# Weight sums made a group ahead, and low parts of streamed weight chunks made by an accumulating load onto the negated high part

## What is computed

```python
x = layer_norm(ALPHA * x + 0.5 * swiglu(x, ffn1_w_up, ffn1_w_down), ln1_g, ln1_b)
h, new_buf, S_new = mixer(x, pos, conv_buf, S0, w_in, conv_w, w_conv_br, w_ret_br, w_out)
x = layer_norm(ALPHA * x + h, ln2_g, ln2_b)
x = layer_norm(ALPHA * x + 0.5 * swiglu(x, ffn2_w_up, ffn2_w_down), ln3_g, ln3_b)

def swiglu(x, w_up, w_down):
    a, b = jnp.split(x @ w_up, 2, axis=-1)
    return (jax.nn.silu(a) * b) @ w_down
```

## Time and profile before

| what | us |
|---|---|
| median of 3 runs | 1880.46 |
| lowest and highest | 1879.18, 1884.25 |
| the profiled execution | 1879.75 |
| its span, first to last instruction | 1877.9 |
| PE busy (share of the span) | 1786.2 (95%) |
| DVE busy | 1445.9 (77%) |
| ACT busy | 674.4 (36%) |
| POOL busy | 641.2 (34%) |

### The profile page before, as it was taken

One profiled execution on the slowest core, in us unless ns is written; L12 is line 12 of the kernel. 1 busy time (PEld: TensorE's weight loads), 2 busy tenths in 40 slices (PEclk: granted clock), 3 DMA queues, 4 the chain that ended last, 5 costly groups with the idle time before them and its releaser, 6 DMA issues. The chain is left out here.

```text
span 1877.9 us, 27089 instructions
## 1 busy us (share of the span) xinstructions
PE 1786.2 (95%) x10680; PEld 1654.4 (88%) x10680; DVE 1445.9 (77%) x1860; ACT 674.4 (36%) x1160; POOL 641.2 (34%) x427
## 2 busy tenths in 40 slices
PE   9979797989999999999999999999999989898898
PEld 9959696979999999999998989888889878788797
DVE  7978787778988777787266777787868878787976
ACT  5415151424344454444105050505224424232333
POOL 3433334353242222222242323131442444343531
PEclk9989998999999999999999999999999999999999
DMA  8746473753454343433674949495951747464633
GB/s 305 224 135 205 143 222 115 224 168 101 180 157 135 99 138 102 146 105 99 236 254 150 336 150 348 154 329 221 362 178 57 224 148 222 138 218 140 190 111 101
DMA packets 99038, 341.34 MB, mean 182 GB/s; under 512 B 9953, under 2 KB 10337, under 8 KB 98401
## 3 DMA queue, kind: packets, MB, share of 16 engines
q1 hardware_dynamic: 51552, 185.36, 28.9%
q0 software_dynamic: 22192, 81.27, 15.7%
q10 hardware_dynamic: 25168, 72.99, 10.7%
HBM read 298.35 MB, written 75.83 MB: 199 GB/s over the span
## 5 line engine op out<-in xcount | busy, mean ns | idle before, releaser
L852 POOL TENSOR_TENSOR wl<-raw,wh 128x1024 fp32r<-128x1024 f32 x124 | 327.4, 2644 | 146.3 <-DMA wh<-in_weights 48.8
L983 PE MATMUL ps<-th,wql 128*128 128x320 f32 x1136 | 351.3, 309 | 1.9 <-ACT pu L1705 1.9
L983 PE MATMUL ps<-th,wqh 128*128 128x320 f32 x1136 | 350.7, 309 | 0.0
L983 PE MATMUL ps<-tl,wqh 128*128 128x320 f32 x1136 | 350.0, 308 | 0.0
L878 POOL TENSOR_TENSOR quad_s<-qraw 128x512 f32<-128x512 f32 x71 | 98.0, 1380 | 605.8 <-DVE wql L2187 386.8
L983 PE MATMUL ps<-xh,wql 128*128 128x320 f32 x852 | 263.4, 309 | 0.8 <-DVE ct L2187 0.5
L983 PE MATMUL ps<-xl,wqh 128*128 128x320 f32 x852 | 262.7, 308 | 0.0
L983 PE MATMUL ps<-xh,wqh 128*128 128x320 f32 x852 | 262.6, 308 | 0.0
L1705 ACT ACTIVATE pu<-ps 128x320 f32<-128x320 f32 x213 | 93.0, 437 | 441.5 <-PE ps L983 441.5
L2187 DVE TENSOR_TENSOR wql<-qraw,wqh 128x512 fp32r<-128x512 f32 x213 | 249.8, 1173 | 0.4
L2187 DVE TENSOR_TENSOR wql<-quad_s,wqh 128x512 fp32r<-128x512 f32 (+1 forms) x213 | 199.0, 934 | 47.0 <-ACT wqh L1705 46.3
(11 more groups left out here) (294 smaller groups left out, 3816.2 us busy)
## 6 DMA issues: line engine op xcount, KB each, us to landing
qraw<-in_quads SPq DMA_DIRECT2D x142, 512.0 KB, 3.7
raw<-in_weights SPq DMA_DIRECT2D x92, 512.0 KB, 5.1
wh<-in_weights POOLq DMA_DIRECT2D x84, 512.0 KB, 5.8
raw<-sums_scratch SPq DMA_DIRECT2D x32, 512.0 KB, 3.7
wh<-sums_scratch POOLq DMA_DIRECT2D x32, 512.0 KB, 5.7
state<-in_state_ret ACTq DMA_DIRECT2D x32, 512.0 KB, 7.7
out_ret_sample<-state ACTq DMA_DIRECT2D x32, 512.0 KB, 5.1
sums_scratch<-in_sum_add POOLq DMA_DIRECT2D x8, 1024.0 KB, 10.0
```

The costliest lines, as they stand in the source:

```text
L852: pool.tensor_tensor(w_lo(r), w_raw(r), w_hi(r).bitcast(f32), ALU.subtract).then_inc(chunk_split, 1)
L983: ins = nc.tensor.matmul(out, lhs, rhs, start=start, stop=stop, skip_group_check=adds)
```

## The change

**Low parts.** For the chunks that are not in BY_ACT, SP no longer loads raw. POOL waits for the high part, writes its negative into wl (line 851 of the new kernel), waits for that instruction, and issues a DMA that loads the plain numbers with an add onto what stands in wl (line 854), so that wl becomes raw - wh. Each slot has a semaphore low_loaded, for which PE waits instead of chunk_split. The nine BY_ACT chunks keep the load by SP and the subtraction.

**Sums.** The adds for a group are issued one group earlier: those of the first group before the loop, those of group n+1 inside group n. ACT's base_copy moves with them: it now stands behind the last quad of a group, for the group two later, and once behind the first quad of all. The last of the three adds now stands among the down products, between the loads of A22's high part and the low part of S3. The calls of high, low and sums in the loop stand in another order.

**SP.** Its queue now holds the quads' loads almost alone; it waits no more for chunk slots or for the sums, except for the BY_ACT chunks.

```diff
@@ -686,8 +688,9 @@
                 for _ in range(n):
                     c = ck.at
                     r = slot_of(c)
-                    slot_free(sync, c)
-                    sync.dma_start(w_raw(r), chunk_source(sync, c)).then_inc(raw_loaded[r], 16)
+                    if c in BY_ACT:
+                        slot_free(sync, c)
+                        sync.dma_start(w_raw(r), a["weights"][PLAIN[c]]).then_inc(raw_loaded[r], 16)
                     ck.add()
 
             def load_quad(stage):
...
@@ -724,13 +727,9 @@
                     load(FIRST_UNITS)
                 load(2)
                 for g in SPLIT_GROUPS:
-                    load(1)
-                    load_quad(2 * k)
-                    load_quad(2 * k)
-                    load(1)
-                    load_quad(2 * k)
-                    load(2)
-                    load_quad(2 * k)
+                    for _ in range(4):
+                        load(1)
+                        load_quad(2 * k)
                     load(3)
                 load(2)
                 load_quad(2 * k)
...
@@ -844,16 +842,23 @@
                 c = ck.at
                 high(c + 1)
                 r = slot_of(c)
-                pool.wait_ge(raw_loaded[r], 16 * loads_of_slot(c))
                 if c in BY_ACT:
+                    pool.wait_ge(raw_loaded[r], 16 * loads_of_slot(c))
                     pool.wait_ge(hi_made, BY_ACT.index(c) + 1)
+                    pool.tensor_tensor(w_lo(r), w_raw(r), w_hi(r).bitcast(f32), ALU.subtract).then_inc(chunk_split, 1)
                 else:
                     pool.wait_ge(hi_loaded[r], 16 * high_loads_of_slot(c))
-                pool.tensor_tensor(w_lo(r), w_raw(r), w_hi(r).bitcast(f32), ALU.subtract).then_inc(chunk_split, 1)
+                    pool.tensor_scalar(w_lo(r), w_hi(r).bitcast(f32), -1.0, None, ALU.mult).then_inc(high_negated, 1)
+                    nk.add()
+                    pool.wait_ge(high_negated, nk())
+                    pool.dma_start(w_lo(r), chunk_source(pool, c), accum_op=ALU.add,
+                                   max_dma_last_dim=4 * D).then_inc(low_loaded[r], 16)
                 ck.add()
 
             def add_first(at):
 
+                if at == SPLITS:
+                    return
                 pool.wait_ge(base_copied, 16 * (at + 1))
                 pool.dma_start(a["sums"][at, 0:2].rearrange("m p d -> (m p) d"),
                                a["sum_add"][at].rearrange("m p d -> (m p) d"), accum_op=ALU.add,
...
@@ -907,24 +914,28 @@
                 high(ck(2))
                 low()
                 low()
+                if k == 0:
+                    add_first(0)
                 sums(2 * k)
+                if k == 0:
+                    add_next(0, 1)
+                    add_next(0, 2)
                 for g in SPLIT_GROUPS:
-                    at = split_after(k, g)
-                    high(ck(1))
+                    following = split_after(k, g) + 1
+                    high(ck(3))
                     sums(2 * k)
-                    add_first(at)
                     low()
                     sums(2 * k)
-                    add_next(at, 1)
+                    add_first(following)
+                    low()
                     high(ck(2))
                     sums(2 * k)
-                    add_next(at, 2)
-                    high(ck(3))
                     low()
+                    add_next(following, 1)
                     sums(2 * k)
                     low()
-                    low()
                     high(ck(2))
+                    add_next(following, 2)
                     low()
                     high(ck(2))
                     low()
...
@@ -1001,10 +1012,12 @@
                 return b
 
             def chunk():
-                s = slot_of(ck.at)
+                c, s = ck.at, slot_of(ck.at)
                 ck.add()
-                if ck() > FIRST_HI:
-                    pe.wait_ge(chunk_split, ck(-FIRST_HI))
+                if c in BY_ACT:
+                    pe.wait_ge(chunk_split, BY_ACT.index(c) + 1)
+                elif c >= FIRST_HI:
+                    pe.wait_ge(low_loaded[s], 16 * high_loads_of_slot(c))
                 return s
 
             def idle_products(n, b):
...
@@ -1874,8 +1887,10 @@
                 for g in range(1, len(GROUPS)):
                     for q in range(4):
                         quad(QUAD_START[2 * k] + 4 * (g - 1) + q)
-                        if q == 2 and g in SPLIT_GROUPS and split_after(k, g) < 2 * len(SPLIT_GROUPS) - 1:
-                            base_copy(split_after(k, g) + 1)
+                        if q == 0 and (k, g) == (0, 1):
+                            base_copy(1)
+                        if q == 3 and g in SPLIT_GROUPS and split_after(k, g) + 2 < SPLITS:
+                            base_copy(split_after(k, g) + 2)
                     if (k, g) == (1, 1):
                         act.dma_start(a["y_prompt"][0:ADDED * 128, :], a["ln3_b"].to_broadcast([ADDED * 128, D])
                                       ).then_inc(y_biased, 16)
```

More of the change, by code:

```diff
@@ L39 @@
 SUMS_KEPT = ("S1", "S3", "S2", "S4")
+SPLITS = 2 * len(SPLIT_GROUPS)
 SPLIT_BANKS = 8
@@ L138, in loads_of_slot @@
 def loads_of_slot(c):
-    return sum(SLOTS[e] == SLOTS[c] for e in range(FIRST_HI, c + 1))
+    return sum(SLOTS[e] == SLOTS[c] and e in BY_ACT for e in range(FIRST_HI, c + 1))
 def high_loads_of_slot(c):
@@ L544, in build_layer @@
         hi_loaded = [sem(f"hi_loaded{i}") for i in range(NSPL + 2)]
-        chunk_split = sem("chunk_split")
+        chunk_split, high_negated = sem("chunk_split"), sem("high_negated")
+        low_loaded = [sem(f"low_loaded{i}") for i in range(NSPL + 2)]
         first_loaded = [sem(f"first_loaded{n}") for n in range(len(FIRST_LOADS))]
@@ L763, in projections @@
                 fourth = SECOND + FIRST_UNITS - 1
-                sync.wait_ge(raw_loaded[slot_of(fourth)], 16 * loads_of_slot(fourth))
                 sync.wait_ge(hi_loaded[slot_of(fourth)], 16 * high_loads_of_slot(fourth))
@@ L830, in _ @@
         def _(pool):
-            ck, hk, qk = Count(FIRST_HI), Count(FIRST_HI), Count()
+            ck, hk, qk, nk = Count(FIRST_HI), Count(FIRST_HI), Count(), Count()
             def high(n):
@@ L1941, in _ @@
                 quad_hi_part(PROJ, what)
-            act.wait_ge(chunk_split, FFN_CHUNKS - FIRST_HI)
+            act.wait_ge(low_loaded[slot_of(SECOND - 1)], 16 * high_loads_of_slot(SECOND - 1))
             ln_load(1)
```

## The result

| | before | after |
|---|---|---|
| median of 4 runs, us | 1880.35 | 1932.86 |
| lowest and highest | 1879.18, 1884.25 | 1927.85, 1937.46 |
| profiled span | 1877.9 | 1926.1 |
| mean granted clock | 0.979 | 0.966 |

The ratio is 1.0276, with a 95% interval of 1.0254 to 1.0299: 52.5 us slower, where 6.5 us faster was forecast, and outside the range.

A forecast was written before the change was run, and what follows sets the result against it. PE, busy 1786.2 of 1877.9 us, was taken to bound the kernel, its idle time mostly waits for DVE's z and ct. -23 - 3 + 17.5 + 2 = -6.5 us gave 1873.2, median 1874; range 1845 to 1902.

The forecast's parts named there:

- The stop ahead of S1: PE's wait for ct before the down products' S1 goes in seven groups, 3.3 us each: 23 us gained.
- The negation: POOL's negation of a high part takes 1.3 us, bounds 1.3 to 2.6, as it reads half a subtraction's numbers.
- GpSimd's issues: By the skill's rule, the 121 loads moved to POOL cost perhaps 0.3 us more each where DVE is busy.
- The accumulating load: The low part's adding load lands in 5.5 to 6 us where DMA queues are quiet; bounds 3.7 and 14.0.
- Down products: From S1 to S4's end in eight split groups: S3 starts 6 us earlier, mostly lost again behind the base copy; -3 us.
- supply keeps up: Rival: the accumulating load lands in 5.6 us even beside the base copy, S4 starts at 22 us; about 1830, chance 0.12.
- Starts: Low parts without slack come late: opening +2.5 us, projections +5 and +1, second feed-forward stage +3.5, last chunk and conv +1.5.
- First group: POOL waits in line for the base copy and two adds before the third quad's sums, delaying DVE and PE: +4 us.
- Heads: Low parts in the heads have 5 us to spare: 0 us, with a bound of 5 us a head.
- Clock: One or two of the new stops bring PE's clock down behind them: +2 us.
- Late low parts: Rival: accumulating loads take 11 to 14 us as a rule, delaying heads, conv units and starts; about 1915, chance 0.18.
- the signs listed for "wrong": Negation above 2.4 us, middle landing below 4.5 or above 9, wl waits in heads, DVE over 10 us for POOL's sum.

The follow-up runs named there:

- no_negation: The changed kernel without the negation and its wait, for all but the first eight chunks and the extra slots (wrong numbers): 1927.7 us, ratio to before 1.0261.
- plain_load: The changed kernel with the low part's second load made plain, without the addition (wrong numbers), negation kept: 1876.4 us, ratio to before 0.9984.
- down_by_subtraction: The changed kernel with S3, A22 and S4 of the eight split groups (24 chunks) again loaded raw by SP and subtracted: 1891.9 us, ratio to before 1.0046.
- copy_next: The changed kernel with ACT's base copy moved behind the first quad of the next group: 1936.4 us, ratio to before 1.0295.
- starts_by_subtraction: The changed kernel with the chunks at the four starts again loaded raw by SP and subtracted: 1909.9 us, ratio to before 1.0155.
- heads_by_subtraction: The changed kernel with chunks from the fifth of the projections to the output projection's end loaded raw and subtracted (47 change): 1917.5 us, ratio to before 1.0209.
- lows_alone: The changed kernel with the sums' adds and base copies in the places and order of before, only low parts new: 1952.5 us, ratio to before 1.0366.

## Why the prediction was wrong, point by point

*The stop ahead of S1: right.* PE's wait for ct fell from 26.9 to 1.2 us, 3 to 4.4 us a group; 23 were forecast.

*The negation: mis-sized.* 3.0 us, outside my bounds of 1.3 to 2.6. The step that failed is the one by which half the reads mean half the time. The Trainium skill (GPSIMD Engine Reference, section 3.1) led the same way, to 0.9 to 1.5 us; the trace doesn't agree. It mattered little: no_negation won 5 us. My guess that GpSimd's issues would cost 0.3 us more a load came out in size (0.92 us against plain_load's 0.58), but it goes with the addition, not with where the load is issued.

*The accumulating load: right alone, wrong in company.* 5.4 us at best and 7.1 in the middle; 5.5 to 6 were forecast for quiet queues. What it adds to the DMA engines' work is 1.25 us, where the text had 1.4.

*Down products: this is where it failed.* -3 forecast; measured 282.1 - 248.6 = +33.5, of which down_by_subtraction gives back 38.0. Two steps failed. The first is S3's high part landing at about 5 us: it landed at 9.3, and still at 8.0 in the last group, with neither copy nor add behind it. The rest of the way to the issue was sized rightly in sum (3.2 us, 2.9 forecast), the long negation included. So even the two groups without a base copy behind them start on S3 at 19.7 and 16.9 us, not 14, and lose 3.7 us together where the text had them gain 7.5. The second step is the order of two events: I had the load for S3 issued at 7.9, ahead of the base copy at 12, and it came at 12.5, behind the copy at 10.8. To the 4.6 us of a late issue it added 4 to 5 us of landing (10.1, against 5.4 in the same group of copy_next), and the six groups with a copy lose 29.9 us together instead of 5. My rival "supply keeps up" and the forecast both counted on a copy that S3 doesn't meet; no case of mine had it meet S3 in six groups.

*Starts: mis-sized.* 12 without the first group's 4 and 1.5 for the last chunk and the conv units; starts_by_subtraction says 23.0. By how far PE falls behind the kernel before, the opening cost 7.2 instead of 2.5, the projections 10.9 instead of 6, the second stage 7.9 instead of 3.5: at each place several chunks follow one another, and each negation and load waits for the one before (POOL at 499.97, 503.76, 507.86), while I had priced the first of the row and 1 us for the second.

*First group: somewhat mis-sized.* PE falls 6.4 us further behind the kernel before in this group (at 87 us of before); 4 were forecast. (The 4.4 that come back ahead of S1 there belong to the 23 above.) DVE waited for POOL's sums twice, 3.8 and 4.7 us, and not once 7.

*Heads: wrong.* 0 forecast with a bound of 20; heads_by_subtraction says 15.4. The step that failed is the weight of the additions on busy DMA engines, put at nothing. The text worked out that the DMA share would go from 0.79 to 0.94, and then put no price on it. Measured the share is 0.88, and the same products take 1.8 us more (66.80 against 65.00), none of it in plain_load. The 1.4 us for each load is near: (0.88 x 66.80 - 0.79 x 65.00) / 7 = 1.1.

*Clock.* 2 us forecast for one or two stops. There were 18 of 4.9 us on average, and the mean clock went from 0.979 to 0.966, but PE's busy time rose by 3.6 us only (1786.2 to 1789.8), so the term itself was nearly right.

*Rivals.* "Late low parts" gave 1915 by landings of 11 us as a rule. The side was right; the mechanism was another, since the middle stayed at 7. Of the signs listed for "wrong", two came: the negation above 2.4 us, and waits for wl in the heads, though of 2.9 us in all. The large waits, for wl at S3 and not at A22 or S4, I had not listed.

What stays open: lows_alone lost 69.9 us, where the changed kernel lost 52.5 with the front's gain of some 25 in it. That the low parts alone lose about 70 to 79 fits, but the front and the down phase lean on each other there, and I didn't split them. Nor did a run say why a negation is slower than a subtraction.

## What to carry to other kernels

Replace work on an engine by a second trip of a DMA only for the operands whose slack in the trace is longer than trip, landing and queue together, chunk by chunk; here 32 of 121 had it, and those alone gave 50 us with the base copy out of the way, 12 to 15 with it in place. If the trip adds onto what is there, price what the addition does to every other transfer. Where a forecast rests on two transfers coming in a certain order less than 5 us apart, price the other order as well: here the smaller behind the larger landed 4.7 us later. And ask of each instruction on POOL what it does to DVE before asking what it costs POOL.

## What the runs showed of the hardware

An accumulating load of 512 KB occupies the 16 DMA engines 1.25 us longer than a plain one and lands 2.4 us later in the middle (7.1 against 4.7); its issue takes POOL 0.92 us instead of 0.58. A one-operand instruction of 128x1024 on POOL took 2.77 us with DVE idle, a two-operand one 1.89 to 2.6. A two-operand instruction of DVE stood still for the rest of a subtraction on POOL, up to 2.8 us, and lost 0.8 us or nothing to a negation (0.3 on average over 115). Issued 1.8 us behind a 1 MB copy in HBM, an accumulating load of 0.5 MB landed in 10.1 us, and in 5.4 with the copy elsewhere; in the last two groups and behind them, which have no copy, the middle is 5.8.
